# A 256-token decoder of a state-space, a stick-breaking, a gated-linear and a mixture-of-experts layer: the order of the opening's loads and turns, and the mixer's scores and maxima in one instruction

## The reference

```python
hn = rmsnorm(x, even_norm)                    # x * rsqrt(mean(x*x) + eps) * gain
q, k, v, u = split(hn @ even_w_in)
# state-space mixer: 32 groups of 16 channels, 64 states each
dt = exp(log_dt)
lam = exp(a_re * dt) * (cos(a_im * dt) + i * sin(a_im * dt))
bb = (lam - 1) / a * (b_re + i * b_im)        # b: [group, state, channel]
h = scan(lam, bb @ u);  y = real(c @ h) + d * u
# later, attention of the mixer, 8 heads of 64
logits = q @ k.T + bias[distance]             # causal
p = softmax(logits)                           # exp(logits - max) / sum
```

## Time and profile before

| | |
|---|---|
| median of 3 runs (lowest, highest) | 1317.54 us (1315.72, 1318.56) |
| the profiled execution | 1317.54 us, its span 1315.8 us |
| busy: PE, DVE, ACT, POOL | 1145.8, 695.4, 460.7, 42.9 us |
| moved by DMA | 343.39 MB, mean 261 GB/s |
| mean granted TensorE clock | 0.938 of 2.4 GHz |

### The profile page before, as it was taken

One profiled execution on the slowest core, in us unless ns is written; L12 is line 12 of the kernel. 1 busy time (PEld: TensorE's weight loads), 2 busy tenths in 40 slices (PEclk: granted clock), 3 DMA queues, 4 the chain that ended last, 5 costly groups with the idle time before them and its releaser, 6 DMA issues.

```text
span 1315.8 us, 19000 instructions
## 1 busy us (share of the span) xinstructions
PE 1145.8 (87%) x7676; PEld 870.1 (66%) x7676; DVE 695.4 (53%) x985; ACT 460.7 (35%) x588; POOL 42.9 (3%) x99
## 2 busy tenths in 40 slices
PE   7999999999999999999999999998657656666655
PEld 6878888888998888888998999963212212121211
DVE  7976777778888777776567687541101010101012
ACT  5574333335766343335364545331001010101001
POOL 5510000000000000000000000000000000000000
PEclk9999999999999999999999999989888788778788
DMA  9334555555434465556553546999999999999996
GB/s 239 142 112 135 184 193 192 191 191 172 161 122 155 149 220 186 186 185 203 172 170 103 192 163 227 414 376 412 422 422 422 422 421 422 422 422 422 422 421 251
DMA packets 140887, 343.39 MB, mean 261 GB/s; under 512 B 11922, under 2 KB 101156, under 8 KB 116756
## 3 DMA queue, kind: packets, MB, share of 16 engines
q1 hardware_dynamic: 139036, 337.83, 68.6%
q0 software_dynamic: 1536, 4.33, 1.1%
q10 hardware_dynamic: 248, 0.28, 0.1%
HBM read 341.36 MB, written 2.62 MB: 261 GB/s over the span
## 4 chain that ended last, share of the span: by engine, by line
PE 64%; DMA 22%; DVE 7%; ACT 4%; issue 1%; SPq 1%; ACTq 0%; DVEq 0%; PEldq 0%
DMA ring<-in_w_exp_down_dram 11%; PE ps L1485 11%; DMA ring<-in_w_exp_up_dram 10%; PE ps L1387 10%; PE ps L1389 9%; PE ps L1388 9%; PE ps L1487 6%; PE ps L1934 5%; PE ps L1959 3%; SPq L550 1%; DVE piece_lo L2151 1%; PE ps L1299 1%; PE ps L1254 1%; PE ps L1412 1%; PE ps L1405 1%
## 5 line engine op out<-in xcount | busy, mean ns | idle before, releaser
L2151 DVE TENSOR_TENSOR piece_lo<-ring,piece_hi 128x2048 fp32r<-128x2048 f32 x118 | 266.6, 2284 | 24.6 <-ACT piece_hi L820 24.0
L820 ACT ACTIVATE piece_hi<-ring 128x2048 fp32r<-128x2048 f32 x118 | 223.1, 1913 | 128.1 <-PE ps L1389 76.6
L1934 PE MATMUL ps<-ring,arena 128*32 128x512 f32 x992 | 153.8, 763 | 97.7 <-DMA ring<-in_w_exp_up_dram 55.3
L1485 PE MATMUL ps<-HT_both,piece_hi 128*128 128x512 f32 x640 | 223.0, 394 | 0.0
L1487 PE MATMUL ps<-HT_both,piece_lo 128*128 128x256 f32 x640 | 177.3, 277 | 0.0
L1934 PEld LDWEIGHTS ps<-ring,arena 128*32 128x32 f32 x992 | 41.6, 136 | 203.4 <-issue 202.7
L1485 PEld LDWEIGHTS ps<-HT_both,piece_hi 128*128 128x128 f32 x640 | 120.0, 187 | 27.9
L1487 PEld LDWEIGHTS ps<-HT_both,piece_lo 128*128 128x128 f32 x640 | 120.2, 188 | 0.8
L1387 PE MATMUL ps<-HT_both,piece_hi 128*128 128x256 f32 x368 | 105.5, 287 | 0.0
L1389 PE MATMUL ps<-HT_both,piece_lo 128*128 128x256 f32 x368 | 104.9, 285 | 0.0
L1388 PE MATMUL ps<-HT_both,piece_hi 128*128 128x256 f32 x368 | 104.8, 285 | 0.0
(11 more groups left out here) (484 smaller groups left out, 2004.4 us busy)
## 6 DMA issues: line engine op xcount, KB each, us to landing
ring<-in_w_exp_gate_dram SPq DMA_DIRECT2D x63, 1024.0 KB, 19.1
ring<-in_w_exp_up_dram SPq DMA_DIRECT2D x61, 1024.0 KB, 19.2
ring<-in_w_exp_down_dram SPq DMA_DIRECT2D x57, 1024.0 KB, 16.5
ring<-in_ffn_w_gate_dram SPq DMA_DIRECT2D x22, 1024.0 KB, 5.4
ring<-in_ffn_w_up_dram SPq DMA_DIRECT2D x22, 1024.0 KB, 5.4
ring<-in_ffn_w_down_dram SPq DMA_DIRECT2D x22, 1024.0 KB, 7.3
ring<-in_w_in_dram SPq DMA_DIRECT2D x20, 1024.0 KB, 5.3
ring<-in_odd_w_in_dram SPq DMA_DIRECT2D x12, 1024.0 KB, 5.3
```

The lines of the kernel that those rows point to most:

```text
L820: act.activation(piece_hi[:, h % HI_SLABS, :], ring[:, k % RING, :], ACT.Copy).then_inc(hi_made, 1)
L1485: pe.matmul(b, hi[:, kt, c], HT_both[:, :, kt * T:(kt + 1) * T], start=kt == 0, stop=False, skip_group_check=True)
L1934: ins = pe.matmul(ps[own, 2 + up, :], mGT[:, kt, own], w[e][:, k4, :], start=(kt == 0), stop=(kt == KT - 1))
L2151: ve.tensor_tensor(piece_lo[k % RING][:, :], ring[:, k % RING, :], piece_hi[:, h % HI_SLABS, :].bitcast(F32), ALU.subtract).then_inc(split, 1)
```

## The change

The rows are renumbered: those of a, and the first norm's gain, come first (40 of them, `FIRST_ROWS`), the others follow. SP loads the two u pieces right behind x, then the other rows with the q and k gains (15 loads are counted on their semaphore). ScalarE's queue loads log_dt, a and the first gain (4 loads), then both parts of B, each as 16 rows of 8 KB in 16 partitions. GpSimd waits for the first u piece only, and loads C. TensorE makes 12 filler transposes, turns dt with the first 40 rows, block 0 of x, the first part of B (16 transposes of 16x128 into bank 5), block 1 of x, the second part of B, makes 6 more fillers, and starts u; the spread of the roots and the turn of the other rows come behind u's first half. VectorE starts with the first columns and the angles, takes the norm's columns in between, and the inverse root behind the angles; the kept roots and the other columns come ahead of `keep_u(0)`; the input weights read B from `ps`. ScalarE takes the exponential of log_dt first, the squares of block 1 behind its norm columns, and the D copies behind the spread of C.

In the mixer, sum and maximum become one instruction for each span of a head, with no separate maxima; z tile 1 and the scores of heads 4 to 7 follow the split of z piece 4 directly, and the inverse root follows the split of z piece 5.

```diff
@@ -125,10 +125,10 @@
-ROW_NORM = {0: 0, 1: 8, 2: 16, 3: 24, 4: 32, 6: 40, 7: 48, 5: 56}
-ROW_LOADS, MISC_LOADS = 18, 9
+ROW_NORM = {0: 32, 1: 40, 2: 48, 3: 56, 4: 64, 6: 72, 7: 80, 5: 88}
+FIRST_ROW_LOADS, ROW_LOADS, MISC_LOADS = 4, 15, 9
...
-ROW_D, ROW_BGLU, ROW_BALPHA, ROW_QN, ROW_KN, ROW_ARE, ROW_AIM, ROW_FINAL, ROWS = 64, 68, 72, 74, 75, 76, 92, 108, 116
+ROW_ARE, ROW_AIM, FIRST_ROWS, ROW_D, ROW_BGLU, ROW_BALPHA, ROW_QN, ROW_KN, ROW_FINAL, ROWS = 0, 16, 40, 96, 100, 104, 106, 107, 108, 116
@@ -224,8 +224,10 @@
-        rows = arena[0:ROWS, 12160:12288]
-        log_dt, dt_rows = arena[0:16, 12024:12026], arena[0:16, 12032:12160]
+        first_rows = arena[0:16 + FIRST_ROWS, 12160:12288]
+        log_dt, dt_rows = arena[0:16, 12024:12026], first_rows[0:16, :]
+        rows = spare_slab[0:ROWS - FIRST_ROWS, 0:P]
+        b_rows = [arena[0:16, 2048 * i:2048 * (i + 1)].rearrange("p (n c) -> p c n", c=GROUP_CH) for i in range(2)]
@@ -238,7 +240,6 @@
-        braw = MT[:, 0:2, :]
@@ -325,6 +326,7 @@
+        b_turned_in = [ps[:, 5, 256 * i:256 * (i + 1)].rearrange("p (t c) -> p t c", c=GROUP_CH) for i in range(2)]
@@ -335,7 +337,7 @@
-        b_loaded, b_im_loaded, dt_loaded = sem("b_loaded"), sem("b_im_loaded"), sem("log_dt_loaded")
+        b_loaded, b_turned, first_rows_loaded = sem("b_rows_loaded"), sem("b_turned"), sem("first_rows_loaded")
@@ -591,17 +593,20 @@
-            row_loads = [(ROW_NORM[0], a["even_norm"][0]), (ROW_NORM[1], a["ffn_norm"][0]),
+            group("u", w0, 768, 2)
+            row_loads = [(ROW_NORM[1], a["ffn_norm"][0]),
...
+                r -= FIRST_ROWS
...
-            group("u", w0, 768, 2)
-            sp.dma_start(braw[:, 1, :].rearrange("p (j c) -> p j c", c=GROUP_CH),
-                         a["ssm_b_im"][0].rearrange("(j g) n c -> (g n) j c", g=2)).then_inc(b_im_loaded, 16)
+            for r, v in ((ROW_QN, a["q_norm"]), (ROW_KN, a["k_norm"])):
+                r -= FIRST_ROWS
+                for half in range(2):
+                    sp.dma_start(rows[r:r + 1, 64 * half:64 * half + 64], v).then_inc(rows_loaded, 16)
@@ -678,11 +683,7 @@
-            for tb in range(2):
-                pool.wait_ge(x_loaded[tb], 16)
-            pool.wait_ge(rows_loaded, 16 * ROW_LOADS)
-            pool.dma_start(braw[:, 0, :].rearrange("p (j c) -> p j c", c=GROUP_CH),
-                           a["ssm_b_re"][0].rearrange("(j g) n c -> (g n) j c", g=2)).then_inc(b_loaded, 16)
+            pool.wait_ge(loaded[0], 16)
@@ -746,15 +747,19 @@
-            act.dma_start(log_dt, a["ssm_log_dt"][0].rearrange("(j g) -> j g", g=2)).then_inc(dt_loaded, 16)
-            for r, v in ((ROW_QN, a["q_norm"]), (ROW_KN, a["k_norm"])):
-                for half in range(2):
-                    act.dma_start(rows[r:r + 1, 64 * half:64 * half + 64], v).then_inc(rows_loaded, 16)
+            act.dma_start(log_dt, a["ssm_log_dt"][0].rearrange("(j g) -> j g", g=2)).then_inc(first_rows_loaded, 16)
...
-                act.dma_start(rows[r:r + 16, :], v[0].rearrange("(j g) n -> j (g n)", g=2)).then_inc(rows_loaded, 16)
-            def norm_sq(n, src):
-                for tb in range(2):
+                act.dma_start(first_rows[16 + r:32 + r, :], v[0].rearrange("(j g) n -> j (g n)", g=2))\
+                    .then_inc(first_rows_loaded, 16)
+            act.dma_start(first_rows[16 + ROW_NORM[0]:24 + ROW_NORM[0], :], a["even_norm"][0].rearrange("(r c) -> r c", c=P))\
+                .then_inc(first_rows_loaded, 16)
+            for i, name in enumerate(("ssm_b_re", "ssm_b_im")):
+                act.dma_start(arena[0:16, 2048 * i:2048 * (i + 1)], a[name][0].rearrange("(j g) n c -> j (g n c)", g=2))\
+                    .then_inc(b_loaded, 16)
+            def norm_sq(n, src, blocks=range(2)):
+                for tb in blocks:
@@ -837,21 +842,18 @@
-            norm_sq(0, X)
-            act.wait_ge(dt_loaded, 16)
+            act.wait_ge(first_rows_loaded, 16 * FIRST_ROW_LOADS)
...
+            norm_sq(0, X, (0,))
...
+            norm_sq(0, X, (1,))
...
-            act.wait_ge(consts_ready, 1)
-            act.wait_ge(ident_ready, 1)
-            for i in range(4):
-                act.activation(lag_w[:, i, 0, :], ident[:, :], ACT.Copy, scale=cols[:, ROW_D + i:ROW_D + i + 1])
@@ -889,6 +891,11 @@
+            act.wait_ge(consts_ready, 1)
+            act.wait_ge(ident_ready, 1)
+            act.wait_ge(cols_ready, 2)
+            for i in range(4):
+                act.activation(lag_w[:, i, 0, :], ident[:, :], ACT.Copy, scale=cols[:, ROW_D + i:ROW_D + i + 1])
@@ -1229,7 +1236,7 @@
-            def norm(n, wait=True, closes=None):
+            def norm(n, wait=True, closes=None, between=None):
@@ -1243,6 +1250,8 @@
+                            if tb:
+                                between()
@@ -1547,15 +1556,33 @@
+            def keep_busy(n):
+                for _ in range(n):
+                    pe.transpose(ps[:, 6, 0:P], ident[:, :], ident[:, :])
...
-            norm(0, wait=False)
-            pe.wait_ge(rows_loaded, 16 * ROW_LOADS)
-            pe.transpose(ps[:, 7, 0:ROWS], rows[:, :], ident[0:ROWS, 0:ROWS])
+            keep_busy(12)
+            pe.wait_ge(first_rows_loaded, 16 * FIRST_ROW_LOADS)
...
-            pe.transpose(ps[:, 7, P:P + 16], dt_rows, ident[0:16, 0:16]).then_inc(cols_full, 1)
-            spread_roots(0)
+            pe.transpose(ps[:, 7, 0:16 + FIRST_ROWS], first_rows, ident[0:16 + FIRST_ROWS, 0:16 + FIRST_ROWS])\
+                .then_inc(cols_full, 1)
+            def turn_b(part):
+                pe.wait_ge(b_loaded, 32)
+                for c in range(GROUP_CH):
+                    ins = pe.transpose(b_turned_in[part][:, :, c], b_rows[part][:, c, :], ident[0:16, 0:16])
+                ins.then_inc(b_turned, 1)
+            norm(0, wait=False, between=lambda: turn_b(0))
+            turn_b(1)
+            keep_busy(6)
...
+            spread_roots(0)
+            pe.wait_ge(rows_loaded, 16 * ROW_LOADS)
+            pe.transpose(ps[:, 7, P:P + ROWS - FIRST_ROWS], rows, ident[0:ROWS - FIRST_ROWS, 0:ROWS - FIRST_ROWS])\
+                .then_inc(cols_full, 1)
@@ -2204,16 +2231,13 @@
-            norm(0, X)
...
-            ve.tensor_copy(cols[:, 0:ROWS], ps[:, 7, 0:ROWS]).then_inc(cols_ready, 1)
-            o.mark(ve.tensor_copy(ssm[:, 1, :], ps[:, 7, P:P + 16]))
+            ve.tensor_copy(cols[:, 0:FIRST_ROWS], ps[:, 7, 16:16 + FIRST_ROWS]).then_inc(cols_ready, 1)
+            o.mark(ve.tensor_copy(ssm[:, 1, :], ps[:, 7, 0:16]))
...
-            norm_columns(0)
...
-            o.mark(ve.tensor_scalar(cols[:, ROW_QN:ROW_QN + 1], cols[:, ROW_QN:ROW_QN + 1], 0.125, None, ALU.mult))
@@ -2223,12 +2247,13 @@
+            norm_columns(0)
...
-            keep_roots(0)
+            norm(0, X)
@@ -2297,10 +2322,14 @@
+            keep_roots(0)
+            ve.wait_ge(cols_full, 2)
+            ve.tensor_copy(cols[:, FIRST_ROWS:ROWS], ps[:, 7, P:P + ROWS - FIRST_ROWS]).then_inc(cols_ready, 1)
...
-            ve.wait_ge(b_loaded, 16)
-            ve.wait_ge(b_im_loaded, 16)
-            b_of = lambda x: braw[:, x, :].rearrange("p (t c) -> p t c", c=GROUP_CH)
+            ve.wait_ge(cols_ready, 2)
+            o.mark(ve.tensor_scalar(cols[:, ROW_QN:ROW_QN + 1], cols[:, ROW_QN:ROW_QN + 1], 0.125, None, ALU.mult))
+            ve.wait_ge(b_turned, 2)
+            b_of = lambda x: b_turned_in[x]
@@ -2587,9 +2616,21 @@
-            moba_bias = lambda h: [(0, T, BT[:, h, :]), (T, 384, BT[:, h, P:T])]
+            spans = ((0, T), (T, 384))
+            def moba_scores(heads):
+                for h in heads:
+                    b = full_tile(ve, "moba_s", h)
+                    for k, (c0, c1) in enumerate(spans):
+                        i = 8 * k + h
+                        ins = ve.tensor_tensor_reduce(S2[:, h, c0:c1], b[:, c0:c1], BT[:, h, T - (c1 - c0):T], 1.0, NEG,
+                                                      ALU.add, ALU.max, sm[:, i:i + 1])
+                    ins.then_inc(emptied["v"], 1)
+                wait_emptied(ve, "moba_s", heads[-1])
...
-            masked_scores("moba", S2, moba_bias, range(4))
+            moba_scores(range(4))
@@ -2602,12 +2643,12 @@
+            by_root("z", 1, sig[1])
+            moba_scores(range(4, 8))
+            ve.tensor_scalar(sm[:, 16:32], sm[:, 0:16], -1.0, None, ALU.mult).then_inc(scored, 1)
+            piece_lo_part("z", 5)
...
-            by_root("z", 1, sig[1])
-            masked_scores("moba", S2, moba_bias, range(4, 8))
-            maxima(S2, 8, spans)
-            piece_lo_part("z", 5)
...
```

## The result

The change makes the kernel slower, by 0.4%. Its median is 1321.15 us (1320.11 to 1322.91, 8 runs) beside 1316.99 us (8 runs) of the kernel before, a ratio of 1.0038 with a 95% interval of 1.0029 to 1.0048. The profiled execution took 1320.38 us (span 1318.4). The prediction was 1316.1, in a range up to 1319.4. The number nearest to the result is that of rival (b), 1321.0.

What follows compares the result with a forecast made beforehand. The opening was taken as bound by VectorE, the mixer by a nearly always busy TensorE. Opening loss 1.8 less mixer gain 3.2 gave -1.4 us, from 1317.54 to 1316.1; range 1313.8 to 1319.4.

Steps and rivals of the forecast that it cites:

- rival (b): Opening: B lands behind u, its transposes hold up VectorE, ScalarE and u; F 14.5, +3.5 us, 1321.0; chance 0.08.
- VectorE's sum behind F: Opening: VectorE's work and waits after F add up so that the input weights begin at F + 15.8.
- F: Opening: the time at which bank 0 of the first norm is full, predicted as 9.6 us.
- The break-even of 7.8 for F: Opening: with F = 7.8 us the input weights would begin at 23.56, as in the kernel before.
- I take 4.5: Opening: landing time assumed for B's loads, from x's slower block; bounds 2.8 and 8.7 us.
- B lands at 7.5: Opening: B, issued at about 2.6 and 3.0, lands at 7.5 us; its transposes then give F = 9.6.
- The first rows are there at 4.95: Opening: first row loads, the last issued from about 2.15, land at 4.95 us, by log_dt's 2.8.
- a loss of 2.5 us: Opening: estimate from the skill's 104 to 109 GB/s, B landing near 8.2; not used in the sum.
- B from PSUM: Opening: input weights reading B from PSUM cost 0, at most 0.1 us for each of four products.
- D copies and GpSimd: Opening: D copies delay ScalarE's chunk copies 0.3 us at most, where it idles; GpSimd issues C about as before.
- u right behind x: Opening: loading u directly after x costs nothing; u should be there when its products need it, at F + 2.1.
- The mixer: Near 709 us: gains 3.2 us, 1.7 from TensorE's shorter idle time and 1.5 from the clock; ends 0 and 3.4.

Runs made afterwards that it cites:

- the run with 3.56 instead of 6.60: Four first row loads on SP's queue ahead of x, against the changed kernel with B in its old form and u late: 1318.78 us, ratio 1.0020.

## Why the prediction was wrong

*VectorE's sum behind F: right.* F + 15.8 is 30.5, the weights began at 30.45. It held within 0.4 in all eleven traces of the new order in which u was in time (F 13.67 and 29.45, 8.93 and 24.59, 17.98 and 33.73), and failed only where u's product was late: 10.47 and 30.50, 8.04 and 28.74, 8.82 and 28.34. The break-even of 7.8 for F was reached by no version.

*"I take 4.5", so "B lands at 7.5": this is the step that failed.* B was usable at 12.05. Its second load was issued at 3.32 instead of 3.0 and took 8.7 us, the upper bound in the prediction's own text. Six traces have the turns of B between the two halves of the norm and waited for B: the turns began at 12.05, 11.46, 11.58, 11.48, 11.49 and 15.31, and F was 14.72, 14.14, 14.25, 14.15, 14.16 and 17.98, each time 2.67 or 2.68 later. The first rows do not move F there: in the first five the exponential starts anywhere from 7.51 to 8.64. So of the 5.1 us by which F was missed, B's landing is 4.5. The other 0.6 is block 1's part up to the full bank, 0.80 instead of 0.23, near the slower pace that I had in hand (228 ns each). The fillers did not prevent that: block 0's transposes, behind 4.67 us of standing still, took 246 ns each at a granted clock of 1.00, so the rows do not say why they were slow.

*"The first rows are there at 4.95": wrong by 3.7, and hidden behind B.* They were usable at 8.64. I took log_dt's landing of 2.8 us for all four, but log_dt is the first load issued and 0.1 KB, and the last of the four is issued 1.4 later, when x's megabyte is under way. Block 0 was turned by 11.32 instead of 6.5 to 7.4, and that is still 0.73 before B. So as the kernel stands, B in time gains little by itself (13.67 with u late, where the rows bound), and the rows in time gain nothing, since F follows B. With B's turns out of the way the rows alone left 11.79, and only the rows ahead of x, with B in its old form, gave 8.85.

*Why B was late.* It is in the queue tables. From 7 to 8 us of the changed kernel, ScalarE's queue, which then carries B:

```profile
q10 hardware_dynamic: 26, 0.12, 90.4%
```

Up to 6 us this queue had moved some 0.02 MB, that is the first rows; nearly all of B went from 6 to 10. From 7 to 8 its 26 packets carried 0.12 MB and took 90% of the time of 16 engines, while from 4 to 5 us x's queue carried 0.40 MB in 101%: a byte of B took three times as long. The Trainium skill (SBUF — State Buffer, "Door 1: The DMA port swizzle") puts a load into partitions 0 to 15 at 104 to 109 GB/s. 0.12 MB in that microsecond is of that size, so the trace agrees, without showing which engine served which load. I had the page's figure beside a loss of 2.5 us and kept the likelier-looking sum; both were too small, since in neither did B's data begin to move only at 6 us, behind x and the rows, and then share the engines with u.

*B from PSUM: right.* Two of its products take 2.33 to 2.38 us against 2.44 from SBUF. *D copies and GpSimd: right,* they cost nothing that shows. *u right behind x: not free,* B's loads took 1.0 to 2.6 us longer with it, and F was 0.5 to 1.0 earlier without it. SP has 15 row loads instead of 12, not 16 instead of 13, and nothing hangs on that.

*The mixer: right in mechanism, near in size.* 3.2 predicted; 3.6 and 4.5 measured in two sets. By the traces the idle time gave 2.1 (1.7 predicted) and the clock 1.5 (1.5 predicted), the latter only against a run in which the clock had fallen. With the new mixer it stayed at 1.00, and no second wait took the place of the first.

*What the sum did not have at all* is the 1.5 us between 77 and 82. No part of the change is there. No view of the kernel before showed it, because there the block border lies behind the 55th matmul, which is due at about the time when the block is ready (71.2 and 71.0).

*The chances.* Rival (b) had the mechanism in the main: B lands late, and TensorE's queue stands still with it, to an F of 14.5. Its reason, u, is only a part, since with u late F was still 13.67. That the total also came out at its 1321.0 is partly luck: it had neither the 1.5 us of the block borders nor the 0.4 more in the mixer, and the stretch behind norm 7 happened to be 1.9 shorter in the trace. It got 0.08 because I reasoned against it from the shape of b_im's load instead of asking how any load fares beside x. The bounds of F in my own text reached 13.8 to 15.8; the range did not, as it should have.

## What to carry to other kernels

How long a small load took to land depended here on what was issued ahead of it and beside it. Take it from a row of a load issued at the same moment, and where no row has it, carry both bounds into the range. If a chain of work begins with small loads, issue them ahead of the large one, as the run with 3.56 instead of 6.60 shows. An engine that executes in order turns a late operand into a stall of everything behind it: B's turns, needed 15 us later, were put in front of the norm and of u, and whichever load of B was late took these with it. When two late loads stand one behind the other, read the last wait first: mending the other gains nothing. And after adding instructions to an engine, look for gaps that wait for nothing where its shortest instructions stand.

## What the runs showed that was not expected

By the spacing of the gaps and the packets, TensorE's instructions come in blocks of 128 matmuls with their weight loads, some 16 KB each. Where matmuls start every 15 ns, a block's border cost up to 0.83 us, and the next one, behind it, 0.70 to 0.97, and whether it does depends on the count of instructions ahead of it: 50 added matmuls in idle time cost the kernel before 1.8 us in the trace. What starts the packet of a block was not tried, and stays open.

Four small loads, 20 KB in all, had landed 1.4 us after the start of the last issue with x behind them (three traces), 4.4 to 4.5 after it with x beside them (two traces), and 5.3 to 6.4 with x, u and B (six traces of the same loads).

An idle time of TensorE of 1.9 us was followed by a granted clock of 0.50 in two traces and of 1.00 in a third, with the same work around it.
